# A two-layer decoder trunk on one core: bias-table product moved to the first MLP, one queue for the first loads, three PSUM rooms for low-rank tiles

## Chip, cores and metric

The kernel runs on one core of one Trainium2 chip. The metric is the device time of one execution in microseconds (us), lower is better. The engines are TensorE (PE, matmuls), VectorE (DVE), ScalarE (ACT), GpSimd (POOL) and SyncE (SP, which only issues transfers). ACT issues transfers too, from the same instruction stream as its arithmetic. PE writes to PSUM, from which ACT and DVE evacuate the products.

## What is computed

A decoder with 1024 positions, width 1024, f32. Layer 0 has latent attention (low-rank queries and keys) and forgetting attention; layer 1 has dilated and sparse attention with a bias by distance. Each layer goes on with an MLP of 4096 hidden columns and a gate.

```python
# layer 0
c_q, c_kv, k_r, fq, fk, fv, f_logit = split_cols(hn @ w_in, EVEN_IN_SIZES)
q = (rms_norm(c_q, q_norm) @ w_uq)        # rank 256
kv = (rms_norm(c_kv, kv_norm) @ w_ukv)    # rank 128
# layer 1, three places
logits = logits + bias_table[t5_bucket(dist)]
# each layer
h = h + rms_norm(mix, norm_mix_post[i])
hn = rms_norm(h, norm_mlp_pre[i])
m = jnp.square(jax.nn.relu(hn @ w_mlp_up[i])) @ w_mlp_down[i]
```

The bias table has 32 rows (buckets) and 16 columns (heads). The kernel multiplies it once by a one-hot matrix, which gives one bias row a head, and writes shifted copies of these rows to DRAM. They are first read in layer 1.

## The kernel before

The work is written out engine by engine in one program; semaphores order it, and each engine takes its instructions in the order of the text. Activations lie transposed: partitions are features, columns are positions, in chunks of 128 features (H, XH, XL and so on, eight chunks).

A product of f32 values is made of three f32r passes: high x high, high x low, low x high (three_pass, line 1311 on). A weight tile of 512 KB is loaded by SP into RAW (two slots; weights, line 833), split by POOL into WH and WL (lines 1124 and 1126), and used by PE. An output tile of 128x1024 takes 16 products of 512 columns for each of the three passes where the inner size is 1024 (48, at line 1318), 12 where it is 256 and 6 where it is 128. A load of RAW waits only until the tile two before it is split.

PSUM has eight banks: ACC (two rooms of two banks, a tile each), TR (two banks) and OP (two banks). A tile gets the room `no % 2` and PE waits until the tile two before it is evacuated (evacuated, line 1306).

The names of the stretches, in order: in0a (tiles cq 0 to 2 and misc), in0p, in0d, in0b, in0c (projections of layer 0), up0 (low-rank tiles), attention "even", out0, then the MLP in eight groups (mlpa0 the first, mlp0 the six between, mlpz0 the last), ple0, gate0; then layer 1 likewise. In the first tile pair of in0a and of mlpa0 PE runs chunk by chunk behind ACT, which makes XH and squares (high, line 1840; square, line 1813), and DVE, which makes XL (low, line 2188). Sums of squares are matmuls by ones (line 1453 into TR; lines 1461, 1462, 1479 and 1492 into OP); root (lines 1831 to 1836) makes the factor from them.

The part that the change touches:

- Start: SP issues the bias table, the one-hot matrix, five tables (lines 826 to 830) and H's chunks 0 and 1, then the weights of in0a. ACT issues the other six chunks of H and the positions. PE makes the three bias tiles first (line 1756), ACT copies them to BRS (line 2040), SP stores BRS (line 1015), waits, and issues five skewed DRAM copies (line 1020), each row of a copy one element further along than the next. After that SP issues the weights of in0p.
- up0: eight tiles of 12 products (uqn, uqr) and eight of 6 (ukt, ukv, ukw). ACT evacuates uqn and ukv, DVE uqr and ukw, and of ukt ACT the high and DVE the low half (lines 1882 and 2322). ACT issues all stores, those of ukt (y_mlav, line 1885) after DVE's part. The buffers UP are a ring of eight. SP then loads VS (values of a job) and BIAS for attention.
- Entry of the MLP: after out0 PE makes the sums (line 1492), ACT the root, DVE adds to H (lines 2205, 2208), ACT and DVE make XH and XL.

Of the kernel before, what the change touches and what calls it, by code (L numbers as in the profile page):

```python
# [15 lines left out]
F32 = mybir.dt.float32  # L16
# [5 lines left out]
P = 128  # L22
S = 1024
# [60 lines left out]
EXTRA = {"in0a": [("brow", 0), ("brow", 1), ("brow", 2)], "in1c": [("gt", 0)]}  # L84
# [11 lines left out]
DVE_RELEASES = {"cq", "misc", "foxv", "foxs", "odd", "odds", "oddk", "dil", "up", "down", "gate", "uqr", "ukw", "ukt"}  # L96
SPLIT = {"foxs", "foxv", "odds", "oddk"}
# [170 lines left out]
def build_attention():  # L268
# [3 lines left out]
    n = dict(load=0, bias=[0, 0], head=[0, 0], raw=0, ops=0, mask=0, rl=0, spread=0, fin=0, xl=0, cor=0, xo=0, whole=0)  # L272
    phases = {}
    for name, plan in (("even", EVEN_JOBS), ("odd", ODD_JOBS)):
        ph = Phase()
        ph.name, ph.jobs, ph.tasks = name, [], []
        for kind, pair in plan:
# [14 lines left out]
            n["load"] += {"loaded": 3, "ring": 2, "spare": 2}.get(j.values, 0) * (kind not in DILATED)  # L292
            j.load, j.head, j.bias, j.raw, j.ops = n["load"], [0, 0], [0, 0], [0, 0], [0, 0]
# [154 lines left out]
def program(nc, ins, out):  # L448
# [5 lines left out]
    with ctx:  # L454
# [88 lines left out]
        ONEHOT = sb("ONEHOT", [33, BROW_N], 120)  # L543
# [48 lines left out]
        s_const = sem("s_const")  # L592
        s_mask = sem("s_mask")
# [39 lines left out]
        s_load = sem("s_load")  # L633
# [61 lines left out]
        N_CONST = 5  # L695
# [42 lines left out]
        for t in (t for u in segs["up0"].iters[0] for t in u.tiles):  # L738
# [3 lines left out]
            n_up = max(n_up, up_slot[t] + (2 if t.kind == "ukt" else 1))  # L742

# [81 lines left out]
        def _(sp):  # L825
            sp.dma_start(T5[0:32, :], ins["t5"]).then_inc(s_t5, 16)
            sp.dma_start(ONEHOT[:], ins["onehot"]).then_inc(s_t5, 16)
            for dst, key in ((GAINS, "gains"), (CONST, "const"), (IDENT, "ident"), (QKVG, "qkvg")):
                sp.dma_start(dst[:], ins[key]).then_inc(s_const, 16)
            sp.dma_start(KR[:, 0:P], ins["mask"]).then_inc(s_const, 16)  # L830
            load_h(sp, 0)
# [40 lines left out]
            def values_in(j):  # L872
# [8 lines left out]
                for hl, c, n, to in ((0, 0, HD, 0), (1, 0, P, HD), (0, HD, HD, 3 * HD)):  # L881
                    load(VS[:, j.slot, :, to:to + n].bitcast(F32), y[hl, :, :, c0 + c:c0 + c + n], s_load)

            def attention(name):
# [55 lines left out]
                for j in ph.jobs:  # L940
# [9 lines left out]
                    elif j.values:  # L950
# [6 lines left out]
                        if j.values != "kept":  # L957
                            for e in range(2):
                                load(RV[rows_of_head(e)], y_v[0 if j.kind == "sel" else 1], s_load)
                    for e in range(2):  # L960
# [27 lines left out]
                        if j.kind == "fox":  # L988
                            load(BIAS[:, e], y_f[h:h + 1].to_broadcast([P, S]), s_bias[e])
# [22 lines left out]
            weights("in0a")  # L1012

# [1806 lines left out]
```

## Time and profile before

| | us |
|---|---|
| three runs: median, lowest, highest | 2951.21, 2950.11, 2963.64 |
| the profiled execution's own time | 2951.49 |
| its span | 2949.7 |
| busy in it: PE, DVE, ACT, POOL | 2813.8, 1151.1, 833.2, 931.7 |
| mean granted clock of PE | 0.983 of full |

Times in the trace count from the span's start. PE's records are pipelined, so two products of a row overlap a little; PE's clock has two levels, 1.2 and 2.4 GHz. "SPq" and "ACTq" are issues of transfers by SP and ACT, with the time for which the issue held the engine. The chain of waits is followed back from the last instruction to what released each step.

### The profile page before, as it was taken

The numbers are of one execution on the slowest core, as the hardware profiler recorded it, in microseconds if no ns is written. First come the engines' busy times: TensorE is split into PE (matmuls) and PEld (weight loads), VectorE is DVE, ScalarE is ACT, GpSimd is POOL, SyncE is SP. The second block draws the span as 40 slices with busy tenths as digits, with TensorE's granted clock in tenths as the row PEclk, the third lists the DMA queues.
The fourth block names the chain that finished last, engine by engine and source line by source line (L and its number), as shares of the span: only waits on it lengthen the run. The fifth ranks groups of instructions, "written<-read, shape, count | busy, mean of one in ns | idle before, by whom it ended". The sixth has DMA issues, their size and how long they took to land.

```text
span 2949.7 us, 36540 instructions
## 1 busy us (share of the span) xinstructions
PE 2813.8 (95%) x13828; PEld 2290.6 (78%) x13828; DVE 1151.1 (39%) x1837; ACT 833.2 (28%) x1461; POOL 931.7 (32%) x611
## 2 busy tenths in 40 slices
PE   7998899989999999999999999888899999999998
PEld 4797888867888888887778777677588888888867
DVE  3425887334222222225533434685522222222254
ACT  3304777332110001114421222675401110000251
POOL 2331156332333333235322213313333332333432
PEclk9999999999999999999999999799999999999999
DMA  4356633211111111111242223653011111111112
GB/s 157 134 186 228 155 96 86 93 36 43 50 43 49 50 50 43 50 64 43 72 170 101 31 45 39 135 124 119 29 50 51 50 43 50 50 48 45 65 36 79
DMA packets 105220, 227.79 MB, mean 77 GB/s; under 512 B 41379, under 2 KB 53155, under 8 KB 104791
## 3 DMA queue, kind: packets, MB, share of 16 engines
q1 hardware_dynamic: 93224, 181.91, 22.2%
q10 hardware_dynamic: 11872, 44.21, 3.9%
q8 instruction: 80, 1.31, 0.2%
q14 instruction: 44, 0.36, 0.1%
HBM read 188.36 MB, written 41.39 MB: 78 GB/s over the span
## 4 chain that ended last, share of the span: by engine, by line
PE 83%; DVE 8%; issue 3%; ACT 2%; SPq 2%; DMA 2%; POOL 1%; ACTq 0%; DVEq 0%; POOLq 0%
PE ACC L1318 64%; PE ACC L1667 5%; PE OP L1636 3%; PE TR L1603 3%; PE ACC L1589 3%; PE ACC L1430 2%; SPq L1020 1%; DVE T L2205 1%; DVE H L2208 1%; DVE PB L2398 1%; DVE XL L2188 1%; DMA RAW<-in_w 1%; ACT PB L1981 1%; ACT PT L1974 1%; DVE PT L2419 1%
## 5 line engine op out<-in xcount | busy, mean ns | idle before, releaser
L1124 POOL CAST WH<-RAW 128x1024 fp32r<-128x1024 f32 x188 | 199.5, 1061 | 1402.4 <-PE ACC L1318 1343.7
L1318 PE MATMUL ACC<-XH,WH 128*128 128x512 f32 x1728 | 545.8, 397 | 43.9 <-DVE XL L2188 31.9
L1318 PE MATMUL ACC<-XL,WH 128*128 128x512 f32 x1728 | 538.1, 393 | 0.0
L1318 PE MATMUL ACC<-XH,WL 128*128 128x512 f32 x1728 | 537.8, 393 | 0.0
L1126 POOL TENSOR_TENSOR WL<-RAW,WH 128x1024 fp32r<-128x1024 f32 x188 | 459.6, 2445 | 21.6
L1318 PEld LDWEIGHTS ACC<-XH,WH 128*128 128x128 f32 x1728 | 324.8, 190 | 141.7 <-issue 54.6
L1927 ACT ACTIVATE HH<-T 128x1024 fp32r<-128x1024 f32 x64 | 67.9, 1061 | 1138.2 <-DVE T L2230 1138.2
L1318 PEld LDWEIGHTS ACC<-XH,WL 128*128 128x128 f32 x1728 | 328.0, 190 | 69.4
L1318 PEld LDWEIGHTS ACC<-XL,WH 128*128 128x128 f32 x1728 | 327.9, 190 | 69.3
L2237 DVE TENSOR_TENSOR M<-M,ACC 128x1024 f32<-128x1024 f32 x128 | 156.3, 1221 | 481.1 <-PE ACC L1318 478.9
L1318 PE MATMUL ACC<-HH,WH 128*128 128x512 f32 x1024 | 316.6, 390 | 3.3 <-DVE M L2237 3.1
L1318 PE MATMUL ACC<-HL,WH 128*128 128x512 f32 x1024 | 315.3, 389 | 0.0
L1318 PE MATMUL ACC<-HH,WL 128*128 128x512 f32 x1024 | 315.3, 389 | 0.0
L2230 DVE SCALAR_TENSOR_TENSOR T<-ACC,R 128x1024 f32<-128x1024 f32 x64 | 78.4, 1224 | 410.8 <-PE ACC L1318 404.5
L1318 PEld LDWEIGHTS ACC<-HH,WH 128*128 128x128 f32 x1024 | 190.9, 188 | 48.3 <-issue 9.5
L1318 PEld LDWEIGHTS ACC<-HL,WH 128*128 128x128 f32 x1024 | 192.2, 188 | 40.1
L1318 PEld LDWEIGHTS ACC<-HH,WL 128*128 128x128 f32 x1024 | 192.2, 188 | 40.0
L2419 DVE TENSOR_TENSOR PT<-TR,PT 128x384 fp32r<-128x384 f32 (+3 forms) x288 | 148.1, 541 | 70.7 <-ACT PT L1974 69.5
L1589 PE MATMUL ACC<-QK 128*128 128x512 f32 (+3 forms) x672 | 168.8, 368 | 4.5 <-DVE VS L2363 2.8
L1603 PE MATMUL TR<-IDENT,PB 128*128 128x128 f32 x840 | 132.8, 280 | 41.9 <-ACT PB L1981 19.1
L1974 ACT ACTIVATE PT<-TR 128x384 fp32r<-128x384 f32 (+3 forms) x288 | 129.4, 480 | 86.1 <-PE TR L1603 84.9
L1981 ACT ACTIVATE PB<-PB,NML 128x128 f32<-128x128 f32 (+1 forms) x192 | 146.0, 761 | 14.1 <-DVE NML L2398 12.0
(262 smaller groups left out, 3419.9 us busy)
## 6 DMA issues: line engine op xcount, KB each, us to landing
RAW<-in_w SPq DMA_DIRECT2D x203, 512.0 KB, 3.5
QK<-y_odds SPq DMA_DIRECT2D x56, 256.0 KB, 5.7
QK<-y_foxs SPq DMA_DIRECT2D x48, 256.0 KB, 5.6
y_foxs<-HALVES ACTq DMA_DIRECT2D x8, 1024.0 KB, 5.0
y_foxv<-HALVES ACTq DMA_DIRECT2D x4, 1024.0 KB, 4.5
BIAS<-y_f SPq DMA_DIRECT2D x8, 512.0 KB, 7.9
H<-in_xT ACTq DMA_DIRECT2D x8, 512.0 KB, 7.0
y_h<-H ACTq DMA_DIRECT2D x8, 512.0 KB, 2.6
```

The costliest lines, as they stand in the source:

```text
L1124: nc.gpsimd.tensor_copy(WH[:, slot], RAW[:, slot]).then_inc(s_whi, 1)
L1126: nc.gpsimd.tensor_tensor(WL[:, slot], RAW[:, slot], WH[:, slot].bitcast(F32), ALU.subtract).then_inc(s_split, 1)
L1318: mm = nc.tensor.matmul(acc[:, h * HALF:(h + 1) * HALF], w(k), x[:, k, h * HALF:(h + 1) * HALF], start=first and k == k0 and w is ws and x ...
L1589: mm = nc.tensor.matmul(score_bank(t, c0, c1), x, k[:, c0:c1], start=m == 0, stop=m == len(passes) - 1 and not masked)
L1603: tr = nc.tensor.transpose(TR[0:w, g.ring, y * P:(y + 1) * P], prob(t)[:, x * w:(x + 1) * w], IDENT[:])
L1636: mm = nc.tensor.matmul(OP[:, c.half.bank, col + c0:col + c1], v, pt, start=c.opens and n == 0 and hl == 0, stop=c.closes and n == len(ord ...
L1667: mm = nc.tensor.matmul(ACC[:, t.pair, cols], w[:, slot, k * P:(k + 1) * P], x[:, k, cols], start=k == 0 and m == 0, stop=k == DC - 1 and ...
L1974: nc.scalar.activation(PT[:, c.buf, 0, k0:k0 + g.n, m * P:(m + 1) * P], TR[:, g.ring, 0:g.n * P].rearrange("p (k q) -> p k q", q=P), ACT.C ...
L1981: nc.scalar.activation(x, x, ACT.Exp, bias=NM[:, t.col:t.col + 1], scale=-1.0, accum_out=L[:, t.col:t.col + 1]).then_inc(s_exp, 1)
L2230: V_.scalar_tensor_tensor(out=x, in0=ACC[:, t.pair], scalar=0.0, in1=R[:], op0=ALU.max, op1=ALU.mult).then_inc(s_evD, 1)
L2237: V_.tensor_tensor(M[:, t.idx], M[:, t.idx], ACC[:, t.pair], ALU.add).then_inc(s_evD, 1)
L2419: V_.tensor_tensor(lo, TR[:, g.ring, 0:g.n * P].rearrange("p (k q) -> p k q", q=P), hi.bitcast(F32), ALU.subtract).then_inc(s_ptD, 1)
```

## The change

It has five parts. (1) The bias tiles come after out0, ahead of mlpa0; ACT copies them between its root and its first XH, stores them after the last square, and issues the skewed copies after mlpa0's last hidden tile. The one-hot matrix is loaded after the first out tile. Its place in SBUF moves. (2) At the start SP issues everything, in the order of use: first weight tile, gains, H 0 to 3, second weight tile, H 4 to 7, tables, positions. ACT and DVE wait for the gains only. (3) Low-rank tiles take turns in three rooms, the third being TR, and PE waits for the tile three before. (4) The stores of y_mlav are issued by SP, and the first bias loads of attention go ahead of them. (5) The semaphore of the value loads is two, one a slot. In the diff, `aside` is the third bias tile.

```diff
-EXTRA = {"in0a": [("brow", 0), ("brow", 1), ("brow", 2)], "in1c": [("gt", 0)]}
+EXTRA = {"mlpa0": [("brow", 0), ("brow", 1), ("brow", 2)], "in1c": [("gt", 0)]}
...
+LOW_RANK = {"uqn", "uqr", "ukt", "ukv", "ukw"}
...
-        self.pair = 0 if self.mixed else no % 2
+        self.low_rank = kind in LOW_RANK
+        self.nth = prev.nth + 1 if self.low_rank and prev.low_rank else 0
+        turn = self.nth % 3 if self.low_rank else 0
+        aside = kind == "brow" and idx == 2
+        self.pair = 0 if self.mixed else 2 if turn == 2 or aside else (no - self.nth + turn) % 2
+        self.back = 1 if self.mixed else 3 if aside or self.low_rank and self.nth > 1 else 2
...
+        def room(t):
+            return TR[:].rearrange("p h s -> p (h s)") if t.pair == 2 else ACC[:, t.pair]
... SP
-            weights("in0a")
-            sp.wait_ge(s_evA, extras["in0a"][2].act)
-            sp.dma_start(b_rows, BRS[:]).then_inc(s_bd, 16)
-            sp.wait_ge(s_bd, 16)
...
-            skew("sel", 12, SEL_W)
...
+            weights("in0a", slice(0, 1))
+            sp.dma_start(GAINS[:], ins["gains"]).then_inc(s_gain, 16)
+            load_h(sp, 0)
+            load_h(sp, 1)
+            weights("in0a", slice(1, 2))
+            load_h(sp, 2)
+            load_h(sp, 3)
...
+            weights("in0a", slice(2, None))
             weights("in0p")
...
             sp.wait_ge(s_misc, 32)
+            for e in range(2):
+                load(BIAS[:, e], y_f[e:e + 1].to_broadcast([P, S]), s_bias[e])
+            for t in segs["up0"].iters[0][2].tiles[0:4]:
+                sp.wait_ge(s_evA, t.act)
+                sp.wait_ge(s_evD, t.dve)
+                for hl, x in enumerate((UPR[:, up_slot[t] % UP_SLOTS].bitcast(F32), up_buffer(t, 1))):
+                    sp.dma_start(y_mlav[hl, :, 2 * t.idx:2 * t.idx + 2].rearrange("p b f -> p (b f)"), x)\
+                        .then_inc(s_up[(up_slot[t] + hl) % UP_SLOTS], 16)
...
-            weights("out0")
+            weights("out0", slice(0, 2))
+            sp.wait_ge(s_tile, segs["out0"].iters[0][0].tiles_end)
+            sp.dma_start(ONEHOT[:], ins["onehot"]).then_inc(s_t5, 16)
+            weights("out0", slice(2, None))
... PE
-                    vals = [tiles[t.no - (1 if t.mixed else 2)].released()[what] if t.no > 1 else 0 for t in ts]
+                    vals = [tiles[t.no - t.back].released()[what] if t.no > 1 else 0 for t in ts]
...
                 stats_summed(f"m{l}")
+                if l == 0:
+                    bias_rows()
                 weights(f"mlpa{l}", **first_unit(f"h{l}"))
... ACT
-            act.wait_ge(s_const, 16 * N_CONST)
...
+            act.wait_ge(s_gain, 16)
...
-            act.wait_ge(s_bd, 16)
...
                 root(f"m{l}", R)
+                for g, t in enumerate(extras["mlpa0"]) if l == 0 else ():
+                    c1 = min(BROW_N, (g + 1) * S)
+                    act.wait_ge(s_tile, t.no + 1)
+                    nc.scalar.activation(BRS[:, g * S:c1], room(t)[0:16, 0:c1 - g * S], ACT.Copy).then_inc(s_evA, 1)
...
+                tile_loop(f"mlpa{l}", mlp)
+                if l == 0:
+                    for kind, head0, width in (("sel", 12, SEL_W), ("win", 12, WIN_W), ("d1", 0, DIL_W),
...
+                        act.dma_start(b_tile[kind], src).then_inc(s_bd, 16)
```

How the instructions stand at three places (waits in brackets). SP at the start, before (ahead of these rows stand the bias table, the one-hot matrix and five tables):

```order
L820 DMA H<-in_xT 128x2x1024
L842 DMA RAW<-in_w 128x1024 x2
L842 DMA RAW<-in_w 128x1024 [waits s_split] x2
L1015 DMA b_rows<-BRS 16x2944 [waits s_evA]
L1020 DMA b_sel<-b_rows 512x1x1024 [waits s_bd]
L1020 DMA b_win<-b_rows 512x1x640
L1020 DMA b_d<-b_rows 512x1x256 x2
L1020 DMA b_d<-b_rows 512x1x128
L842 DMA RAW<-in_w 128x1024 [waits s_split] x4
```

and with the change:

```order
L848 DMA RAW<-in_w 128x1024
L1020 DMA GAINS<-in_gains 128x80
L832 DMA H<-in_xT 128x2x1024 x2
L848 DMA RAW<-in_w 128x1024
L832 DMA H<-in_xT 128x2x1024 x2
L1027 DMA CONST<-in_const 128x8
L1027 DMA IDENT<-in_ident 128x128
L1027 DMA QKVG<-in_qkvg 128x3
L1028 DMA KR<-in_mask 128x128
L1029 DMA T_140<-in_t 32x16
L1030 DMA POS<-in_positions 128x1024
L848 DMA RAW<-in_w 128x1024 [waits s_split] x6
```

The one-hot matrix, BRS's store and the skewed copies (five, four rows) are gone from the front, and the first weight tile stands first.

SP between up0 and attention, where rows of y_foxv are the values of a job, before (from the loads of job 0) and then with the change:

```order
L842 DMA RAW<-in_w 128x1024 [waits s_split] x3
L847 DMA VS<-y_foxv 128x8x64 [waits s_store0,s_rope,s_store1,s_misc,s_tile]
L847 DMA VS<-y_foxv 128x8x128
L847 DMA VS<-y_foxv 128x8x64
L847 DMA BIAS<-y_f 128x1024 x2
L847 DMA VS<-y_foxv 128x8x64
```

```order
L848 DMA RAW<-in_w 128x1024 [waits s_split] x3
L853 DMA BIAS<-y_f 128x1024 [waits s_misc,s_tile]
L853 DMA BIAS<-y_f 128x1024
L1056 DMA y_mlav<-UPR 128x1024 [waits s_evD,s_evA]
L1056 DMA y_mlav<-UP 128x1024
L1056 DMA y_mlav<-UPR 128x1024 [waits s_evD,s_evA]
L1056 DMA y_mlav<-UP 128x1024
L1056 DMA y_mlav<-UPR 128x1024 [waits s_evD,s_evA]
L1056 DMA y_mlav<-UP 128x1024
L1056 DMA y_mlav<-UPR 128x1024 [waits s_evD,s_evA]
L1056 DMA y_mlav<-UP 128x1024
L853 DMA VS<-y_foxv 128x8x64 [waits s_store1,s_store0,s_rope]
L853 DMA VS<-y_foxv 128x8x128
```

The BIAS loads come first, the y_mlav stores, which stood on ACT, second, the VS loads last.

ACT in mlpa0, with the change (before, the two rows of a hidden tile are followed by those of the next group at once):

```order
L1951 ACTIVATE HH<-T 128x1024 [waits s_evD]
L1953 ACTIVATE T<-T 128x1024 [waits s_hhi]
L1951 ACTIVATE HH<-T 128x1024 [waits s_evD]
L1953 ACTIVATE T<-T 128x1024 [waits s_hhi]
L2128 DMA b_sel<-b_rows 512x1x1024
L2128 DMA b_win<-b_rows 512x1x640
L2128 DMA b_d<-b_rows 512x1x256 x2
L2128 DMA b_d<-b_rows 512x1x128
```

The skewed copies stand between the last hidden tile of mlpa0 and the first of mlp0.

## Rows read from the trace of the kernel before

**Rows 1.** The page: busy share of PE, and the DMA issues by line (section 6).

```profile
PE 2813.8 (95%) x13828; PEld 2290.6 (78%) x13828; DVE 1151.1 (39%) x1837; ACT 833.2 (28%) x1461; POOL 931.7 (32%) x611
...
RAW<-in_w SPq DMA_DIRECT2D x203, 512.0 KB, 3.5
```

**Rows 2.** Timeline of 0 to 60: start us, us, engine line op out<-in xcount [idle before].

```profile
12.48 1.28 ACT L2040 ACT_TABLE_LOAD   x1 [12.48 <-PE ACC L1756]
...
19.45 1.04 POOL L1124 CAST WH<-RAW 128x1024 fp32r<-128x1024 f32 x1 [2.85 <-DMA RAW<-in_w]
...
20.57 2.35 POOL L1126 TENSOR_TENSOR WL<-RAW,WH 128x1024 fp32r<-128x1024 f32 x1
20.81 1.13 ACT L1840 ACTIVATE XH<-H,GAINS 128x1024 fp32r<-128x1024 f32 x1
...
22.80 1.13 ACT L1840 ACTIVATE XH<-H,GAINS 128x1024 fp32r<-128x1024 f32 x1
...
24.15 1.19 PE L1318 MATMUL ACC<-XH,WH 128*128 128x512 f32 x2 [4.18 <-DVE XL L2188]
...
31.07 0.62 PE L1318 MATMUL ACC<-XH,WH 128*128 128x512 f32 x2
...
56.19 1.45 POOL L1124 CAST WH<-RAW 128x1024 fp32r<-128x1024 f32 x1 [5.45 <-PE ACC L1318]
```

**Rows 3.** Timeline of 76 to 104, PE alone.

```profile
79.43 3.59 PE L1479 MATMUL OP<-Q,ONES 128*128 128x512 f32 x8
86.97 1.22 PE L1318 MATMUL ACC<-XH,WH 128*128 128x512 f32 x2 [3.95 <-POOL WL L1126]
...
92.25 0.63 PE L1318 MATMUL ACC<-XH,WH 128*128 128x512 f32 x2
```

**Rows 4.** The chain of waits over 0 to 300: start us, us, what.

```profile
by line: PE ACC L1318 34.8%; PE ACC L1430 15.4%; SPq L1020 13.7%; DMA RAW<-in_w 8.1%; POOL WL L1126 2.7%; issue 2.3%; DVE UP L2322 1.6%; DVE UP L2338 1.6%; PE OP L1636 1.4%; PE TR L1603 1.4%; ACT UPR L1882 1.4%; POOL WH L1124 1.4%; DVE PB L
...
4.64 14.76 DMA RAW<-in_w
...
73.72 9.68 DMA RAW<-in_w
```

**Rows 5.** Timeline of up0 and the start of attention.

```profile
225.31 0.63 PE L1318 MATMUL ACC<-CQH,WH 128*128 128x512 f32 x2
...
269.89 1.22 DVE L2326 COPY UP<-ACC 128x1024 f32<-128x1024 f32 x1 [2.36 <-PE ACC L1318]
...
271.21 0.41 PE L1589 MATMUL ACC<-QK 128*128 128x128 f32 x2 [1.36 <-issue]
...
278.92 0.63 PE L1636 MATMUL OP<-PT,VS 128*128 128x256 f32 x4
```

**Rows 6.** DMA issues of 1490 to 1530: KB each, us to landing.

```profile
W<-in_w SPq DMA_DIRECT2D x2, 2048.0 KB, 10.0
```

**Rows 7.** The tile UP from 225 to 285: ns min/median/max, first and last start us.

```profile
L2322 DVE TENSOR_TENSOR UP<-ACC,UPR x4: 1224/1225/1225, 253.4 to 263.3; 128x1024 f32<-128x1024 f32 x4
```

**Rows 8.** Windows: busy us of PE, PEld, DVE, ACT, POOL, then clock, DMA share, GB/s.

```profile
261.00:264.00 3.00, 2.35 (x6) 1.61 (x6) 0.92 (x2) 1.02 (x1) 0.00 (x0) 0.68 1.04 421
```

**Rows 9.** Timelines where the moved work goes: first its ACT copies today, then its new surroundings.

```profile
15.73 1.92 ACT L2040 ACTIVATE BRS<-ACC 16x1024 f32<-16x1024 f32 x2 [1.97 <-DMA KR<-in_mask]
...
557.17 1.04 POOL L1124 CAST WH<-RAW 128x1024 fp32r<-128x1024 f32 x1 [7.40 <-PE ACC L1318]
...
642.81 1.15 ACT L1840 ACTIVATE XH<-H,GAINS 128x1024 fp32r<-128x1024 f32 x1 [2.67 <-DVE H L2208]
...
645.15 1.28 DVE L2188 SCALAR_TENSOR_TENSOR XL<-H,GAINS,XH 128x1024 fp32r<-128x1024 f32 x1
...
646.57 1.19 PE L1318 MATMUL ACC<-XH,WH 128*128 128x512 f32 x2 [9.95 <-DVE XL L2188]
...
761.25 1.06 ACT L1927 ACTIVATE HH<-T 128x1024 fp32r<-128x1024 f32 x1 [52.85 <-DVE T L2230]
```

**Rows 10.** DMA issues of 0 to 22.

```profile
H<-in_xT SPq DMA_DIRECT2D x1, 1024.0 KB, 14.0
```

More of the change, by code:

```diff
@@ L291, in build_attention @@
             ph.jobs.append(j)
-            n["load"] += {"loaded": 3, "ring": 2, "spare": 2}.get(j.values, 0) * (kind not in DILATED)
-            j.load, j.head, j.bias, j.raw, j.ops = n["load"], [0, 0], [0, 0], [0, 0], [0, 0]
+            n["load"][j.slot] += {"loaded": 3, "ring": 2, "spare": 2}.get(j.values, 0) * (kind not in DILATED)
+            j.load, j.head, j.bias, j.raw, j.ops = n["load"][j.slot], [0, 0], [0, 0], [0, 0], [0, 0]
             for e in range(2):
@@ L988, in attention @@
                         if j.kind == "fox":
-                            load(BIAS[:, e], y_f[h:h + 1].to_broadcast([P, S]), s_bias[e])
+                            if before:
+                                load(BIAS[:, e], y_f[h:h + 1].to_broadcast([P, S]), s_bias[e])
                         else:
@@ L1254, in attention @@
                         merge(j, k)
-            for name in ("in0a", "in0p", "in0d", "in0b", "in0c", "up0"):
+            weights("in0a", units_of=slice(0, 2))
+            pool.wait_ge(s_const, 16 * N_CONST)
+            nc.gpsimd.tensor_copy(IDR[:], IDENT[:]).then_inc(s_ones, 1)
+            nc.gpsimd.tensor_copy(MKR[:], KR[:, 0:P]).then_inc(s_ones, 1)
+            nc.gpsimd.tensor_tensor(PICK[:], IDENT[:, 0:64:32], IDENT[:, 64:128:32], ALU.add).then_inc(s_pick, 1)
+            weights("in0a", units_of=slice(2, None))
+            for name in ("in0p", "in0d", "in0b", "in0c", "up0"):
                 weights(name)
@@ L1729, in hid_ready, with bias_rows @@
                     need(pe, s_hid, [T_SLOTS + u.tiles[0].up - HID_GROUP + k + 1 for u in us], it)
+            def bias_rows():
+                pe.wait_ge(s_t5, 32)
+                pe.wait_ge(s_ones, 2)
+                for g, t in enumerate(extras["mlpa0"]):
+                    evacuated([t], 0)
+                    for h in range(2):
+                        c0 = g * S + h * HALF
+                        c1 = min(BROW_N, c0 + HALF)
+                        mm = nc.tensor.matmul(room(t)[0:16, h * HALF:h * HALF + c1 - c0], T5[:], ONEHOT[:, c0:c1],
+                                              start=True, stop=True)
+                    mm.then_inc(s_tile, 1)
             def layer_end(l):
@@ L1881, in store @@
                         hi = UPR[:, n % UP_SLOTS]
[L1882 to L1886 removed]
+                        nc.scalar.activation(hi, room(t), ACT.Copy).then_inc(s_evA, 1)
                         return
@@ L1890, in store @@
                         up_free(act, t)
-                        nc.scalar.activation(up_buffer(t), ACC[:, t.pair], ACT.Copy).then_inc(s_evA, 1)
+                        nc.scalar.activation(up_buffer(t), room(t), ACT.Copy).then_inc(s_evA, 1)
                         act.wait_ge(s_evA, t.act)
```

100 lines of the change are left out of this document (41 added, 59 removed).

## The prediction

> **What bounds the kernel now.** TensorE (PE) is busy for 95% of the span [rows 1], so a gain can only come from a stretch in which PE stands still, runs at the low clock or does work that can be dropped. I read the chain of waits over the first 300 us for such stretches, then the timeline of each engine inside them, then the DMA list and the table by windows, and last the stretch where the moved work goes. The reader is to see three stretches.
>
> First, PE has its first projection product only at 24.15, and the first pair of projection tiles ends where POOL is released, at 56.19 [rows 2]. Second, after the fourth projection tile PE stands for 3.95 us before in0p and then runs twelve products at the low clock, 1.2 GHz [rows 3]; the chain goes through SP, whose DMA issues of line 1020 make 13.7% of it over these 300 us, 41 us, and then, at 73.72, through the weights of in0p, which take 9.68 us because they stand in the same queue behind the copies [rows 4]. Third, the sixteen low-rank tiles of up0 begin at 225.3 and their last evacuation ends at 271.11 [rows 5]. Their matmuls need eight times 2.72 us and eight times 1.36 us (0.227 us a product of 512 columns), 32.6 us, so 13 us are waits on two PSUM rooms.
>
> **The change, part by part.**
>
> *A, the start.* The bias matmuls leave the front, and one queue loads in order of use. Today weights, inputs and tables share two queues, so the first weight tile lands at 19.4 and ACT starts on H at 20.81 [rows 2, 4]. What a lone queue needs is seen at 1502, where SP issues two loads of 2048 KB that land after 10.0 us on average [rows 6], and in the lone weight load of 512 KB, 3.5 us [rows 1]: both fit 2.2 us plus 0.41 MB a us. SP begins at 0.8. The first weight tile lands at 4.3; POOL's two passes, 1.04 + 2.35 us [rows 2], end at 7.8. The first two input chunks have 1.6 MB ahead of and in them and land at 7.0. The Trainium skill's page "DMA: Bandwidth & Descriptors", section "Anatomy of one DMA", gives about 2.0 us plus bytes over 436 GB/s for the other, software path; by that they land at 6.5 and the sum would be 0.5 us lower. I keep the rows. ACT then loads its table (1.28 us [rows 2]; the load waits for H) and begins at 8.3, where it now begins at 20.81: 12.5 us earlier. From there the stretch is the same: ACT takes 1.99 us a chunk, PE is bound by itself from the fourth chunk (31.07) on [rows 2], and the stretch ends 35.4 us after ACT's start, at 43.7. DVE's low halves collide with POOL's splitting less than now, since the first split is over; without any collision the fourth chunk comes 1.9 us sooner. I take half of that: A = **13.4 us**. Ends: 10 (H lands 2.5 us later than worked out) and 15.5. The later chunks are no limit: the last lands at 16, ACT wants it at 20. The constants behind them land by 19 and are wanted at 33 and later.
>
> *B, the SP queue.* With the skewed copies gone from SP, the weights of in0p are issued as soon as POOL has split the tile before. PE comes straight from the statistics (end 83.0) to in0p: 3.95 us of waiting and twelve products at 0.43 instead of 0.23 us, 2.4, go [rows 3]; with the ramp between, 6.6 us, as the chain shows 13.6 us for 48 products that take 10.9 at 2.4 GHz. B = **6.6 us**; ends 4 and 7. What is late next is DVE, which has CQ ready well before. The skill's same page, section "Issuing engines are not separate DMA queues", says that issuing from another engine saves only issue time, usually small. By that the move would be worth some 2 us, and the sum 4.6 us higher. The rows speak against it here: the issues of line 1020 keep an engine for 40 us, so who issues matters.
>
> *C, three rooms for low-rank tiles.* The stores of y_mlav leave ACT for SP, and tile n waits for tile n-3. Today each ukt tile costs 3.3 us, in a ring of PE, ACT, DVE and ACT's issues: DVE's four parts begin from 253.4 to 263.3 [rows 7]. I replayed the sixteen tiles with the rows' durations (ACT 1.03, DVE 1.23, PE 2.72 or 1.36): PE runs unbroken up to tile 10, ending at 251.2, then DVE's 1.23 us a tile sets the pace; the last tile ends at 260.0 and its evacuation at 261.3 instead of 271.1. That is 9.8 us. Against it stands the DMA: from 252 on it moves 0.41 MB a us [rows 8] and is full in both versions. The first loads of VS were issued at 252 and now stand in SP's queue behind the 4.2 MB of y_mlav, which share with 2.1 MB of y_kn on ACT's. That puts the values of the first job at about 272.6. The first product on values comes 7.7 us after the first logits (278.92 against 271.21 [rows 5]), so it would be asked for at 269.0: a new wait of 3.6 us, in front of everything that PE has behind it. The score bias is loaded ahead, at 247, and costs nothing. C = **6.2 us**; ends 1 (values land 5 us later still) and 9.8 (they come in time).
>
> *D, the bias rows at the MLP's entry.* Six matmuls of 512 columns in f32 are twelve records; four such matmuls take 3.59 us [rows 3], so 5.4 us. They stand where PE waits 9.95 us anyway (to 646.57) [rows 9]. ACT's three copies (0.96 us each; two took 1.92 [rows 9]) come after its root, which ends at 640.14, and end at 643.0, where XH begins at 642.81: 0.2 us late, and DVE wants that result only at 645.15. PE is then idle 4.6 us instead of 9.95; after 3.95 idle us it was at 1.2 GHz too [rows 3], so the clock gains nothing. The b_rows store fits into ACT's wait for statistics. D = **0**. If the cover fails, ACT's 2.8 us are the most it costs.
>
> *E, the skewed copies on ACT.* ACT is held some 41 us from 708.4. It has nothing to do until 761.25, 52.85 us after its last square [rows 9], so 11 us are spare. A weight load is issued once the tile two before it is split, some 20 us before its use, so it can be slowed much. **0**; if the cover is gone, see the rival.
>
> *F, the one-hot load between the weights of out0.* The third weight tile is now issued after the first out tile (557), with 0.4 MB ahead. It lands at 562, POOL takes 3.4 us, and PE wants it at 567.9; today POOL began at 557.17 [rows 9]. 2.5 us are spare. **0**, at worst 3.
>
> Sum: 13.4 + 6.6 + 6.2 = 26.2 us. The profiled execution took 2951.49 for a span of 2949.7 and stands 0.3 us above the median of 2951.21. 2951.5 - 26.2 = 2925.3, say **2925.5 us**. All three stretches are ahead of a chain that PE then carries to the end, so none should be given back. The terms' ends give 15 to 32 us, so 2919 to 2936.5, and F adds up to 3.
>
> **The rivals.** About 0.5% (14.8 us) is what a measurement of this kernel tells from no change.
>
> *The DMA takes the third stretch (15%).* Evacuations wait for the stores of buffers used twice, or values land still later, and C is 0: 2931.5. For it: the full DMA [rows 8]; against: first stores meet an idle queue.
>
> *One queue does not bring H early (11%).* Today's only H load on SP took 14.0 us [rows 10]. If H lands at 14, A is about 6: 2933. Against: its queue then had 4 MB beside it.
>
> *The gain is given back (5%).* F's load takes as long as now at the start, some 7.6 us, PE stands 5 us at out0, and A and C are at their low ends: about 2940.
>
> *ACT is held too long, slower than before (4%).* With the copies on ACT's queue beside weight loads, they might take far longer. The first product on hidden values is wanted at 792, and ACT, DVE need some 5 us before it, so it decides from a return of ACT at 787, that is copies of 79 us instead of 41. For a time above today's they must take over 105 us. At three times today's, 124 us, PE stands 45 us: 2970. For it: these copies are slow (SP held 40 us for 4.6 MB) and the weight load behind them took 9.68 us [rows 4]. Against: different queues share in turn, and there is twice the time.
>
> **How the numbers follow.** The forecast has 65%. It is the likeliest case's sum. Its own range is 2917 to 2934; the first two rivals lie at its upper end. The range 2915 to 2937 leaves out the last two rivals and some of the tails. Faster by over 0.5% means below 2936.5: nearly all of the forecast and most of the first two rivals, 0.90. Within 0.5%: 0.06. Slower: 0.04.
>
> **What the changed profile would show.** First projection product at about 10.8 and first pair done near 43; in0p without a wait behind the statistics, at 2.4 GHz; last evacuation of up0 about 30 us earlier than 271, and a PE wait at the first product on values of some 3 us; bias matmuls inside PE's gap after out0; ACT's copies over before its next HH. The forecast is wrong if H lands after 10, if POOL waits for weights in out0, or if PE has a gap in the second group of the MLP.

## The result and the profile after

| | before | changed |
|---|---|---|
| median of seven runs each, us | 2955.53 | 2934.93 |
| lowest, highest | 2950.11, 2963.71 | 2930.13, 2949.60 |
| the profiled execution, its span | 2951.49, 2949.7 | 2947.39, 2945.6 |
| mean granted clock in it | 0.983 | 0.978 |

The ratio is 0.9937, with a 95% interval of 0.9915 to 0.9958: 12 to 25 us faster. The prediction was 2925.5 us, within 2915 to 2937, so the time lies in the range, 9.4 us above the forecast. The profiled execution of the changed kernel is one of its two long ones, and only 4.1 us shorter than before. So I follow the chain of work in it, place by place, and say at the end where it lost the rest.

**The start.** Timelines of 0 to 60 of the changed kernel, and its DMA issues of 0 to 22 (KB each, us to landing):

```profile
4.60 1.04 POOL L1136 CAST WH<-RAW 128x1024 fp32r<-128x1024 f32 x1 [3.48 <-DMA RAW<-in_w]
8.35 1.28 ACT L1868 ACT_TABLE_LOAD   x1 [8.35 <-DMA H<-in_xT]
9.64 1.15 ACT L1868 ACTIVATE XH<-H,GAINS 128x1024 fp32r<-128x1024 f32 x1
12.26 1.19 PE L1336 MATMUL ACC<-XH,WH 128*128 128x512 f32 x2 [12.26 <-DVE XL L2219]
44.48 1.45 POOL L1136 CAST WH<-RAW 128x1024 fp32r<-128x1024 f32 x1 [5.45 <-PE ACC L1336]
```

```profile
H<-in_xT SPq DMA_DIRECT2D x4, 1024.0 KB, 10.1
```

Against [rows 2] the first product comes 11.9 us earlier (12.26 for 24.15) and POOL's release behind the first pair 11.7 us earlier (44.48 for 56.19). H's four loads take 10.1 us at the median, where the one on SP took 14.0 [rows 10]. The brackets tell what holds ACT now: the arrival of H, at 8.35, then the function table.

**Between the statistics and in0p.** Timeline of PE, 65 to 110:

```profile
67.71 3.59 PE L1501 MATMUL OP<-Q,ONES 128*128 128x512 f32 x8
70.74 1.03 PE L1336 MATMUL ACC<-XH,WH 128*128 128x512 f32 x2
```

No bracket: PE goes from one to the other without standing still, where [rows 3] has 3.95 us of waiting for POOL. The next tiles stand 18.4 us ahead of before, so this place gave 6.7.

**up0 and the first job of attention.** Timelines of SP, then of DVE and PE, the chain of waits, and a row by windows:

```profile
228.90 0.80 SPq L853 DMA_DIRECT2D BIAS<-y_f  x2
240.92 1.21 SPq L1056 DMA_DIRECT2D y_mlav<-UP  x1
242.65 14.55 SPq L853 DMA_DIRECT2D VS<-y_foxv  x6
```

```profile
241.32 1.22 DVE L2357 COPY UP<-ACC 128x1024 f32<-128x1024 f32 x1 [1.52 <-PE ACC L1336]
242.65 0.41 PE L1611 MATMUL ACC<-QK 128*128 128x128 f32 x2 [1.36 <-issue]
257.49 1.08 PE L1658 MATMUL OP<-PT,VS 128*128 128x256 f32 x4 [7.00 <-DMA VS<-y_foxv]
```

```profile
243.45 3.70 SPq L853
...
247.20 10.16 DMA VS<-y_foxv
```

```profile
255.00:261.00 6.00, 3.51 (x13) 3.25 (x14) 0.89 (x2) 1.73 (x4) 0.00 (x0) 0.50 0.83 193
```

SP issues the two bias loads at 228.90, long ahead of their use. The last evacuation of up0 ends at 242.54 where [rows 5] have 271.11: 28.6 us ahead, so up0 itself became 10.2 us shorter. Eight microseconds later PE stands for 7.00 us. The chain names why: SP turned to the value loads only at 242.65, behind the last store of y_mlav; it reached the third one at 247.20, and that one landed 10.16 us after its issue. The last line is the table by windows: behind the wait PE's clock is 0.50 of full, 1.2 GHz. At out0 the kernel is 19.9 us ahead (its first product at 525.93 for 545.86). That is 1.5 us more than the 18.4 ahead of up0: of the 10.2 us some 1.5 are left.

**Out0 and the entry of the MLP.** Timelines of SP, POOL, PE and ACT:

```profile
537.13 0.36 SPq L1064 DMA_DIRECT2D ONEHOT<-in_onehot  x1
543.76 1.04 POOL L1136 CAST WH<-RAW 128x1024 fp32r<-128x1024 f32 x1 [13.93 <-DMA RAW<-in_w]
```

```profile
616.62 3.67 PE L1763 MATMUL ACC<-ONEHOT,T 33*16 33x512 f32 x8
620.09 3.19 PE L1763 MATMUL TR<-ONEHOT,T 33*16 33x512 f32 x4
626.73 1.19 PE L1336 MATMUL ACC<-XH,WH 128*128 128x512 f32 x2 [3.45 <-DVE XL L2219]
```

```profile
620.12 1.90 ACT L2111 ACTIVATE BRS<-ACC 16x1024 f32<-16x1024 f32 x2
623.32 0.91 ACT L2111 ACTIVATE BRS<-TR 16x896 f32<-16x896 f32 x1 [1.30 <-PE TR L1763]
624.13 1.13 ACT L1868 ACTIVATE XH<-H,GAINS 128x1024 fp32r<-128x1024 f32 x1
```

The weights behind the one-hot load are split by 547.3 and wanted at 547.9. The bias products fill 6.7 us of PE's gap of 9.95; the last four records, 3.19 us, ran at 1.2 GHz (granted clock 0.50), and ACT waited 1.30 us for them. ACT's first XH so began 1.2 us late (624.13 where 642.81 less the lead of 19.9 is 622.9). It ended at 625.26 and DVE's XL began at 625.29, hardly later than before: the slack was just used up. PE's first MLP product stands 19.84 us ahead of [rows 9], 0.1 less than at out0.

**The skewed copies.** Timeline of ACT, 680 to 745:

```profile
687.49 0.74 ACTq L2128 DMA_DIRECT2D b_sel<-b_rows  x1
688.27 10.00 ACTq L2128 DMA_DIRECT2D b_win<-b_rows  x1
698.30 35.84 ACTq L2128 DMA_DIRECT2D b_d<-b_rows  x3
741.41 1.06 ACT L1951 ACTIVATE HH<-T 128x1024 fp32r<-128x1024 f32 x1 [52.86 <-DVE T L2261]
```

They hold ACT until 734.1 and its next work is at 741.41, 19.84 us ahead of before like all around it.

**What the profiled run lost later.** In layer 1 a row of 64 narrow products (64 columns; two records each) stands between wide ones, line 1334 before and 1352 now. PE, before, then changed:

```profile
1566.14 7.33 PE L1334 MATMUL OP<-CBF,W 128*128 128x64 f32 x64 [0.93 <-issue]
1573.30 7.31 PE L1334 MATMUL TR<-CBF,W 128*128 128x64 f32 x64
```

```profile
1547.50 13.02 PE L1352 MATMUL OP<-CBF,W 128*128 128x64 f32 x64 [0.92 <-issue]
1560.32 13.86 PE L1352 MATMUL TR<-CBF,W 128*128 128x64 f32 x64
```

The same work at 1.2 GHz: the granted clock over 1547 to 1575 was 0.53 of full. With the slow products behind it this costs 14.6 us: by 1588 PE is 4.0 us ahead of before instead of 18.6. Nothing of the change is near. It is an event of single executions: of the 65 runs of the kernel before that stand beside all results here, 13 took over 2960 us and none between 2956 and 2960; of the changed kernel's seven, two took 2947 and 2950. Of the experiments below, e6 was profiled in a long run too (2950.40), and these two rows take 13.05 and 13.86 us there; in all others that have the rows unmixed (e1 to e5, e9, e11, e12), none of them a long run, each takes 7.3 us. So the change is worth what the chain shows up to there, some 19 to 20 us; the shortest runs differ by as much, 2930.13 for 2950.11.

### The profile page after: what moved, and what is told of

Its sections match the earlier page's. It is cut to its first block, busy times and chain, and to the rows that moved or that the text cites. A ratio compares the mean times of both kernels' runs of the same rounds, so it can differ in the third digit from the quotient of the medians.

```text
span 2945.6 us, 36545 instructions
## 1 busy us (share of the span) xinstructions
PE 2817.8 (96%) x13828; PEld 2303.0 (78%) x13828; DVE 1147.5 (39%) x1837; ACT 832.4 (28%) x1461; POOL 930.0 (32%) x611
## 4 chain that ended last, share of the span: by engine, by line
PE 85%; DVE 8%; issue 3%; ACT 2%; DMA 1%; SPq 1%; POOL 0%; DVEq 0%; ACTq 0%; POOLq 0%
PE ACC L1336 65%; PE ACC L1689 5%; PE OP L1658 3%; PE TR L1625 3%; PE ACC L1611 2%; PE ACC L1450 2%; DVE T L2236 1%; DVE XL L2219 1%; DVE H L2239 1%; DVE PB L2429 1%; ACT PB L2005 1%; ACT PT L1998 1%; DVE PT L2450 1%; PE TR L1475 1%; PE ACC L1584 1%
## 6 DMA issues: line engine op xcount, KB each, us to landing
H<-in_xT SPq DMA_DIRECT2D x4, 1024.0 KB, 10.1
```

## The experiments

Each was timed beside the kernel before, on the same chip; e5 to e8 on another chip than the rest, where the kernel before took 2953.11 (18 runs) for 2954.87 and 2954.26 (19 and 21 runs). Since the long runs blur a median of few, I read the trace of each kernel at the same four places:

| kernel | POOL's fourth cast | first logits | first product of out0 | from the first column to the third | median, us (runs) |
|---|---|---|---|---|---|
| before | 56.19 | 271.21 | 545.86 | 489.7 | 2955.53 (7) |
| changed | 44.48 | 242.65 | 525.93 | 481.5 | 2934.93 (7) |
| e1 values first | 45.07 | 243.23 | 518.49 | 473.4 | 2923.99 (4) |
| e2 two rooms | 43.63 | 247.02 | 529.19 | 485.6 | 2937.12 (10) |
| e3 stores on ACT | 43.79 | 249.23 | 523.83 | 480.0 | 2933.30 (4) |
| e4 copies on SP | 44.20 | 242.36 | 527.20 | 483.0 | 2954.14 (10) |
| e5 two queues | 49.33 | 247.50 | 532.21 | 482.9 | 2936.46 (5) |
| e6 early table | 43.89 | 242.06 | 526.99 | 483.1 | 2932.02 (10) |
| e11 second job waits | 44.73 | 242.90 | 526.22 | 481.5 | 2933.39 (10) |
| e12 copies alone | 57.11 | 265.75 | 540.30 | 483.2 | 2947.46 (10) |

Kernels that are alike between the first and the third column (changed, e4, e5, e6, e11) took 481.5 to 483.1 there, so a difference of 1.6 us in this column can be chance.

### e1: the values ahead of half the stores

```diff
-            for t in segs["up0"].iters[0][2].tiles[0:4]:
+            for t in segs["up0"].iters[0][2].tiles[0:2]:
                 ... the stores of y_mlav
             sp.wait_ge(s_rope, ROPE_KEY_STEPS + 2)
...
+            fetch_values(phases["even"].jobs[0])
+            for t in segs["up0"].iters[0][2].tiles[2:4]:
+                ... the stores of y_mlav
```

> The changed kernel, with one thing in another order: SP issues the value loads of the first job after two of the four y_mlav tiles (after the last of the rope steps, 231.4) instead of after all four (242.65). My theory: the 7.0 us wait of PE at the first product on values is there because these loads stand behind the stores in SP's queue. Then they are issued near 236, land before the product asks for them (250.5), the wait goes with the 1.2 GHz that follows it, and out0 starts 7 to 8.5 us earlier than 526.17, near 518; the fastest run is near 2922 where the changed kernel's is 2930. Rival: the DMA engines are the bound in this stretch (stores of y_mlav and y_kn beside them), the loads land no earlier than 254 and the gain is under 4 us. Second rival: the stores that now come last keep buffers of the ring, low-rank tiles are evacuated later, and the last evacuation of up0 moves from 242.5 to 246 or later, which eats half of it.

Timelines of SP and PE:

```profile
237.70 4.60 SPq L853 DMA_DIRECT2D VS<-y_foxv  x3
```

```profile
251.58 0.63 PE L1666 MATMUL OP<-PT,VS 128*128 128x256 f32 x4
```

The product on values has no bracket any more and runs in 0.63 us instead of 1.08, at the full clock. The last evacuation of up0 did not move (logits at 243.23, its start being 0.6 later). The values were loaded by the loop of attention before; now that loop leaves out the first job's. The column gives 8.0 us less, the median is 2923.99 (2923.22 to 2924.58), ratio 0.9882 (0.9857 to 0.9907). Both rivals fall; the wait was one of order in a queue. The loads were no quicker, 6.6, 9.8 and 10.7 us to landing: the third landed at 251.0, half a microsecond before PE wanted it at 251.58, so there is little to spare.

### e2 and e3: the rooms and the stores apart

```diff
# e2
-LOW_RANK = {"uqn", "uqr", "ukt", "ukv", "ukw"}
+LOW_RANK = set()
# e3: the stores of y_mlav leave SP, and on ACT behind its high half
+                        act.wait_ge(s_evD, t.dve)
+                        for hl, x in enumerate((hi.bitcast(F32), up_buffer(t, 1))):
+                            act.dma_start(y_mlav[hl, ...
```

> The changed kernel with low-rank tiles in two rooms again; the stores of y_mlav stay on SP. My theory: the ring of 3.3 us a ukt tile in the kernel before was made mostly by the stores in ACT's own stream (ACT waits for DVE before it issues), less by the number of rooms. With two rooms and the stores on SP a room turns in 1.36 + 1.03 + 1.23 us, 1.8 us a tile, so the last evacuation of up0 is at 245 to 248 instead of 242.5 (kernel before, less what its start was later: 252.7). The value loads are then issued 3 to 5 us later too, so PE's wait of 7 us at the first product on values stays, and out0 starts 3 to 5 us later than 526.17. Rival: the rooms are the whole of it, the last evacuation is at 251 or later. Second rival: the value loads are bound by the DMA engines, land when they do now, and out0 starts when it does now.

> The changed kernel with the stores of y_mlav back in ACT's stream, three rooms kept. My theory: ACT again waits for DVE in every ukt tile, 3.3 us a tile, so the last evacuation of up0 is near 250 to 252 instead of 242.5; SP issues the value loads at 231.5, they land before 250, and PE does not wait at the first product on values. The two cancel: out0 starts within 2 us of 526.17, that is, third rooms and the queue's order together were worth next to nothing. Rival: three rooms let PE run ahead of ACT, the last evacuation is at 245, no wait behind it, and out0 starts 4 us or more earlier than in the changed kernel.

In e2 the logits start 203.4 us behind the fourth cast instead of 198.2, so the third room alone is worth 5.2 us at that place. PE's longest wait in up0, and its wait for values, in the timeline of e2:

```profile
235.54 0.47 PE L1401 MATMUL ACC<-WH,CQH 128*128 128x512 f32 x1 [2.32 <-DVE UP L2353]
258.88 1.09 PE L1658 MATMUL OP<-PT,VS 128*128 128x256 f32 x4 [5.47 <-DMA VS<-y_foxv]
```

Up to out0 2.5 to 4.1 us of the 5.2 are left, since the wait for values is 1.5 us shorter. In e3 the stores hold ACT's stream again, 3.3 to 3.8 us a ukt tile:

```profile
234.42 1.03 ACT L1904 ACTIVATE UPR<-ACC 128x1024 fp32r<-128x1024 f32 x1 [2.30 <-issue]
236.73 0.33 ACTq L1907 DMA_DIRECT2D y_mlav<-UPR  x1
237.09 1.02 ACTq L1907 DMA_DIRECT2D y_mlav<-UP  x1
238.21 1.02 ACT L1904 ACTIVATE UPR<-ACC 128x1024 fp32r<-128x1024 f32 x1 [2.76 <-issue]
```

The logits come 205.4 us behind the fourth cast, 7.3 later than in the changed kernel; SP issues the values at 230.71 and PE does not wait for them. Out0 comes 1.5 to 3 us earlier. So moving the stores won 7 us of up0 and lost as much or more at the next place: the first theory of e3 holds, with out0 2.3 us earlier where it said within 2. e12 below has neither piece of C and takes 483.2 us from the fourth cast to out0. Against it the stores' move alone loses 2.4 us (e2, 485.6), the third room alone, with the bias loads ahead, gains 3.2 (e3, 480.0), both gain at most 1.7 (481.5 to 483.1), and both with the values in front gain 9.8 (e1, 473.4). It is the move of the stores that pays only with the values in front.

### e4: the copies on SP again, but in the MLP

```diff
-            for name in ("mlpa0", "mlp0", "mlpz0"):
+            weights("mlpa0")
+            sp.wait_ge(s_bd, 16)
+            for kind, head0, width in (("sel", 12, SEL_W), ...
+                sp.dma_start(b_tile[kind], src).then_inc(s_bd, 16)
+            for name in ("mlp0", "mlpz0"):
                 weights(name)
```

> The changed kernel with the five skewed copies issued by SP, after the weight loads of mlpa0 and ahead of those of mlp0, instead of by ACT. My theory (it is the step of my prediction that prices the SP queue): the issues hold whatever engine makes them for some 41 to 47 us; SP's next weight load is then issued that much later, has some 14 us to spare, and PE stands 25 to 33 us in the MLP once, so the time is 25 to 35 us over the changed kernel, 2957 to 2965 at its fastest, slower than the kernel before. Rival, the Trainium skill's page on DMA bandwidth and descriptors: issuing from another engine saves only issue time, usually small; then PE has no gap there and the time is that of the changed kernel.

Timelines of SP, POOL and PE:

```profile
700.33 32.07 SPq L1072 DMA_DIRECT2D b_d<-b_rows  x3
733.18 63.19 SPq L848 DMA_DIRECT2D RAW<-in_w  x8
```

```profile
742.12 1.04 POOL L1143 CAST WH<-RAW 128x1024 fp32r<-128x1024 f32 x1 [30.12 <-DMA RAW<-in_w]
```

```profile
746.00 1.19 PE L1343 MATMUL ACC<-XH,WH 128*128 128x512 f32 x2 [15.89 <-POOL WL L1145]
```

SP was held 42.1 us (690.32 to 732.40), POOL sat idle for 30.12 us instead of some 7.4, and PE stood 15.89 us and then ran some ten products at 1.2 GHz. The trace from out0 to layer 1 is some 19 us longer than in the other kernels (1038.5 for 1017.7 to 1021.6), and the median is 19.2 us over the changed kernel's. The 25 to 33 expected were too many: SP's next load could go only when the tile cast at 697.27 was split, near 700.7, so the first 10 of the 42 us lay in a time when SP would have waited anyway. But the sign is plain. The Trainium skill's page "DMA: Bandwidth & Descriptors", section "Issuing engines are not separate DMA queues", says that issuing from another engine saves only the sequencer's time to initiate the DMA, "usually small relative to the DMA itself". This trace differs: initiating held SP for 42.1 us of about 52 that the 4608 KB were under way, and who carries it decides over 19 us.

### e12: the copies alone, from the kernel before

The five copies go from SP to ACT behind mlpa0's last hidden tile; the bias products stay in front.

> The kernel before with one part of the change alone: the five skewed copies are issued by ACT after mlpa0's last hidden tile, all else is as before (bias products in front, two queues, two rooms). My theory (steps B and E): the weights of in0p are issued as soon as POOL has split the tile two before, PE's wait of 3.95 us and the twelve slow products go, in0p starts and ends 6.6 us earlier, and nothing else moves: 6 to 7 us less than the kernel before, fastest run near 2943. Rival: another releaser stands just behind the weights at in0p (DVE's CQ, or the first product's room), and less than 4 us is left. Second rival: the other copies of the start still sit in SP's queue and it gains nothing.

PE's wait at in0p went. PE's timeline there, 76 to 104:

```profile
83.35 1.03 PE L1309 MATMUL ACC<-XH,WH 128*128 128x512 f32 x2
```

Fourth cast to out0 is 483.2 instead of 489.7, and the median 2947.46 against 2954.26 of the kernel before in the same series. That is **6.5 to 6.8 us** for step B. It is shown by the trace; the times alone do not tell it from no change (ratio 0.9992, 0.9977 to 1.0007). ACT, held for 46.6 us here, was not late in the MLP (HH again behind 52.86 us of idle time): step E alone costs nothing.

### e5 and e6: the start

```diff
# e5: H's chunks 2 to 7
-            load_h(sp, 1)
             weights("in0a", slice(1, 2))
-            load_h(sp, 2)
-            load_h(sp, 3)
+            for m in range(1, 4):
+                load_h(act, m)
# e6, ACT, ahead of its wait for the gains
+            act.wait_ge(s_ones, 1)
+            nc.scalar.activation(BRS[0:1, 0:1], ONES[0:1, 0:1], ACT.Square)
```

> The changed kernel with H's chunks 2 to 7 issued by ACT at its start, as in the kernel before, and all the rest of the new order on SP. My theory (step A): what the start gained came from the order, and the DMA engines are near full from 4 us on, so transfers that begin together slow each other: the first two chunks of H land 2 to 4 us later than 8.3, PE's first projection product moves from 12.26 to 14 to 16 and the first pair of tiles ends 1.5 to 4 us later, the time is that much longer. Rival: one lone queue does not fill the DMA engines so early in the program, two queues start faster, H lands at 8.3 or sooner, and the first pair ends when it does now or up to 1 us earlier.

> The changed kernel with one more instruction on ACT: a square of one element as soon as POOL has set the ones, so that ACT's function table (1.28 us, at 8.35 behind the arrival of H) is loaded while the first transfers are under way. My theory: the table is on the path from H's landing to XH, so XH begins at 8.4 instead of 9.64, PE's first projection product comes at 11.0 instead of 12.26 and the first pair of tiles ends 1.2 us earlier; the time falls by 1.2 us, which only the trace can show. Rival: after the first chunk the later landings of H or the first weight tile's low half (8.05) hold the stretch, and less than 0.4 us is gained.

Timeline of ACT and DMA issues in e5:

```profile
12.70 1.28 ACT L1865 ACT_TABLE_LOAD   x1 [12.70 <-DMA H<-in_xT]
```

```profile
H<-in_xT ACTq DMA_DIRECT2D x3, 1024.0 KB, 10.8
H<-in_xT SPq DMA_DIRECT2D x1, 1024.0 KB, 10.9
```

With a second queue H's first chunks land at 12.70, 4.4 us later, and the fourth cast comes at 49.33, 4.9 us later: the theory, somewhat over its numbers. ACT's first load of H, issued at 0.89, landed at 7.2 and its second at 12.2; the load on SP, issued at 1.68 behind them and wanted first, landed at 12.6. e5's five runs (2935.27 to 2936.65) lie 5 us over the changed kernel's shortest.

In e6 the table is loaded at 0.91, and XH begins when H lands (8.28). From that landing to the fourth cast it is 35.6 us; in the four kernels with this edit 35.1 to 35.6, in the eight without it 36.1 to 36.9. So it is worth **1.1 us**, and no median shows it: e6 ran 2929.17 to 2950.40.

### e11: do the second job's loads slow the first's?

```diff
+                if j.no == 1:
+                    sp.wait_ge(s_load[0], 16 * 3)
```

> The changed kernel, SP waiting with the value loads of the second job until the three of the first have landed. In the changed kernel the third load of the first job (256 KB) took 10.16 us, where such loads take 4.4 us later in attention. Theory one: the stores of y_mlav and y_kn issued just ahead of it slow it; then nothing changes, PE's wait at the first product on values stays at 6 to 7 us. Theory two: the second job's three loads (1 MB in pieces of 256 and 512 bytes) behind it take half of the DMA engines from it; then it lands 3 to 5 us earlier, and PE's wait falls to 2 to 4 us. I expect the first for two thirds of it: a wait of 5 to 6 us.

Chain of waits, and PE's row:

```profile
247.29 10.19 DMA VS<-y_foxv
```

```profile
257.61 1.09 PE L1660 MATMUL OP<-PT,VS 128*128 128x256 f32 x4 [6.75 <-DMA VS<-y_foxv]
```

Not at all: 10.19 us with nothing behind it, 10.16 with a megabyte. Whatever slows this load was issued before it; that it is the stores alone was not shown apart.

### e7, e8, e10 and e9: the narrow products, and the sum

```diff
# e7: in the first tile of in1c, ahead of chunk k
+                    if k < 4:
+                        compress(k)        # 16 narrow products
# e10: group 0 ahead of weights("in1c"), the others
+                    if 1 <= k < 4:
```

> The changed kernel with the 64 products of layer 1's block compression (64 columns each, 14.5 us in one row) put in four groups of 16 between the chunks of the next weight tile's products of 512 columns; two small groups behind them come one third into the tile after. My theory: the runs of both kernels fall in clusters some 13 us apart since the row of narrow products lets the granted clock fall to 1.2 GHz in some executions (in the changed kernel's profile 13.0 and 13.9 us for the two halves, in the kernel before 7.3 each). Mixed with wide ones the clock stays, no run lies over 2940, the median is 2930 to 2933, and the stretch from the first narrow product to the end of the next wide tile takes 26 us. Rival: the clock falls at random or for what other parts of the chip do, and a third or more of the runs still lie 13 us over the fastest. Second rival: the clock falls in another place instead, or the later compression makes attention of layer 1 wait, and the fastest run is over 2933.

> The value loads after two stores, the early function table and the mixed narrow products together, on the changed kernel. My theory: the three are in different stretches that PE's chain runs through one after the other, so they add: 8 us, 1.2 us and the upper cluster of the runs; median 2920 to 2923, against 2955 of the kernel before. Rival: a saving is given back at a later wait, and the median is 2925 or more.

> The value loads after two stores and the early function table, narrow products left in one row, on the changed kernel. My theory: the value order is worth 8 us, the table 0.6 to 1.2 us, and mixing the narrow products in the way tried before cost 3 to 5 us (PE waited 2.17 us for a room in front of them, which the row of narrow products had covered, and the clock fell behind that wait). So the fastest run is at 2921 to 2922.5, the median at 2922 to 2924 unless more than half the runs fall into the upper cluster 13 us above. Rival: the mixing cost nothing, and this kernel lies at 2926 to 2929 too.

> As the kernel with value order and early table, and the narrow products mixed with wide ones in another way: the first group of 16 in front of the wait for the room, the other three after the first, second and third chunk. My theory: PE does not stand for 2.17 us at the low clock any more, the stretch up to the transposes of layer 1 ends 3 us earlier than in the first mixed version (1591.73), and no run falls into the upper cluster: fastest 2922 to 2924, highest under 2928. Rival: groups of narrow products between wide ones cost by themselves (change of pace, a dip of the clock in some group), and the fastest run stays at 2925 or above.

The first groups in e7, then in e10:

```profile
1545.06 4.89 PE L1349 MATMUL OP<-CBF,W 128*128 128x64 f32 x32 [2.17 <-DVE HALVES L2318]
1552.41 4.57 PE L1349 MATMUL OP<-CBF,W 128*128 128x64 f32 x32
```

```profile
1535.96 6.15 PE L1357 MATMUL OP<-CBF,W 128*128 128x64 f32 x32 [0.93 <-issue]
1544.58 6.92 PE L1357 MATMUL OP<-CBF,W 128*128 128x64 f32 x32
```

At full clock a group takes 3.68 us. In e7 PE first stood for a room (2.17 us), which the row of narrow products had covered. In e8's profile, an ordinary run of it, the first group took 7.06 us behind a wait of 2.16. In e10 that wait is gone, and in the profiled run, its longest, the first two groups ran slow nevertheless: mixing does not keep the clock. Of the 16 runs of e7, e8 and e10 none lies 13 us over its kernel's shortest, but two lie 8 and 11 over; of the unmixed kernels' runs, before's included, about one in five did. By that share none in 16 would still come in some 3 of 100 cases, so it hints at fewer long runs and does not show it; what makes the clock fall in one run and not in the next stays open. e7 is at best 2935.11, 5 us worse than the changed kernel at its best; e8 2928.35 (2926.05 to 2929.33), where 2920 to 2923 was expected.

Without the mixing e9 has 2923.53 (2920.58 to 2928.05), ratio 0.9906 (0.9892 to 0.9921); e10 has 2923.78 (2919.99 to 2931.45). e1, e9 and e10 can't be told apart by their medians. All three beat the changed kernel by some 11 us, and the kernel before by 30. I would keep e9: by the trace its two edits add, and it leaves layer 1 alone.

## Why the prediction was right, and where it was off

**What bounds the kernel** held: three stretches, and a chain that PE carries to the end. The 19.9 us at out0 are still 19.84 at the MLP and 18.6 at 1547; from out0 to there the profiles of all kernels but e4 took 1017.7 to 1021.6 us, so the last 1.2 are within chance.

**A, the start: 11.7 us in the profiled run, 13.4 predicted.** The weights were right (POOL at 4.60, predicted 4.3). H landed at 8.35 and not at 7.0: that is 1.35 of the 1.7 us. In ten other profiles with this order it landed at 7.2 to 9.9, mostly near 7.3, so the fit was 0.3 us short and the profiled run one of the later ones. The estimate from the Trainium skill's page "DMA: Bandwidth & Descriptors", section "Anatomy of one DMA", which is for the software path, was 6.5. The trace has 8.35, further from it than from the rows' 7.0. From ACT's first XH to the end of the pair it took 34.8 us for 35.4 before: of the 1.9 us that I had halved, 0.5 came. e5 shows that the order in one queue, and not only the absence of the bias products, makes the gain. The ends 10 and 15.5 held it.

**B, the SP queue: 6.7 us in the profile, 6.5 to 6.8 in e12, 6.6 predicted.** The reading of line 1020 as time in which an engine is held is confirmed twice, by e12 and, with the opposite sign, by e4.

**C, three rooms: 1.5 us, 6.2 predicted; this is the step that failed, by its second half.** "That is 9.8 us" was 10.2. "A new wait of 3.6 us" was 7.00 and a slow restart, which together took 8 to 9 us back. The wait stood where the text put it, at the first product on values, which came 7.8 us after the logits as said (7.7). Mis-sized was the landing of the values: from the end of up0 I had them after 11.3 us (272.6 against 261.3) and they took 14.8. I had reckoned with one common rate of 0.41 MB a us for all that was in flight. The changed kernel by windows (the last two figures are the DMA engines' busy share and GB/s), and value loads issued between 300 and 500 (KB each, us to landing):

```profile
251.00:254.00 3.00, 0.00 (x0) 0.00 (x0) 1.15 (x4) 0.47 (x2) 0.95 (x1) 1.00 0.99 256
254.00:257.00 3.00, 0.00 (x0) 0.00 (x0) 0.00 (x0) 0.00 (x0) 0.00 (x0) 0.63 1.02 207
```

```profile
VS<-y_foxv SPq DMA_DIRECT2D x2, 256.0 KB, 4.3
VS<-y_foxv SPq DMA_DIRECT2D x1, 512.0 KB, 5.1
```

The DMA engines were busy all the time, and moved 0.26 and 0.21 MB a us, not 0.41. The last store landed at 252.4, so from there on only values were in flight, in pieces of 256 and 512 bytes; that the short pieces make the rate low fits this, but was not tried apart. The first job's three loads took 11.7, 12.2 and 10.2 us to landing, where such loads take 4.3 to 5.1 us later in attention. And the restart behind the wait, at 1.2 GHz, I had left out, though I had priced the same thing in B. What came, 1.5 us, is near the end that I gave, 1 us, though the values landed 3.5 us later and not 5; the restart made up for the difference. e1 shows that the wait was avoidable; e3 that without the stores' move it is not there at all.

**D, the bias rows: 0.1 us.** The cost came as predicted, but only just. 5.4 us were predicted for the products and they took 6.7, since the last four ran at 1.2 GHz. I had let ACT copy without a wait; it waited 1.30 us for them, so XH was 1.2 us late and not 0.2. DVE's slack covered 1.1 of it, and PE's first MLP product lost 0.1.

**E, the copies on ACT: 0.** ACT was held for 46.6 us instead of 41, of 53.9 until its next work.

**F, the one-hot load: 0, but by 0.6 us** where I saw 2.5 to spare: the weight tile behind it took 6.2 us.

The rival "the DMA takes the third stretch" (C = 0, 2931.5) is nearest to what happened. Of its two ways, evacuations that wait for stores did not come; "values land still later" is what did. "One queue does not bring H early", "the gain is given back" and "ACT is held too long" fell.

**The time.** The sum of the parts measured is 11.7 + 6.7 + 1.5 - 0.1 = 19.8 us, where 26.2 were predicted; the medians differ by 20.6 and the shortest runs by 20.0. So the forecast gain was 5.6 us too large by the medians and 6.4 by the trace, of which 4.7 are C and 1.7 A. The other 4.0 of the 9.6 us between 2925.3 and 2934.93 are the base: I started from 2951.5, and the kernel before has 2955.53 as the median of seven. That the time still lies in the range is owed to its width of 22 us and does not speak for C.

## What to carry to other kernels

When stores move to a queue that also issues loads, list what is issued behind them and when it is wanted; the load that the next stage wants first goes ahead of the stores that nobody waits for yet. Price an issue by how long its engine is held in the trace, and give long ones to an engine with a gap longer than that. A long wait of PE cost its length and then the products at 1.2 GHz behind it (7.00 us became 8 here, 15.89 some 19), so count both.

## What the runs showed of the hardware that I had not expected

- The five copies from DRAM to DRAM (4608 KB, in rows of 512 to 4096 bytes) held the issuing engine for most of the time that they ran: 42.1 us of about 52 on SP in e4, 46.6 us of about 56 on ACT. The first and largest issue held ACT for 0.74 us, the second, behind it, for 10.00. In e4, with nothing beside them from 701 to 731, they moved 103 GB/s at a mean busy share of the DMA engines of only 0.26. Each copy's pattern has four rows outermost; whether another order of its dimensions would use more of the engines was not tried.
- The first load of H on a lone queue landed at 7.2 to 9.9 us in eleven profiles of kernels with the same order at the start.
- 64 products of 64 columns in a row take 14.5 us or 26.7, by the execution, at 2.4 or 1.2 GHz; the two profiles with the slow rows are both of long runs, 17 and 21 us over the shortest of their kernels.
